# Spreading each expert's rows over the partitions, with two output accumulators and another gather order, in a mixture-of-experts layer step

## What is computed

```
scores = sigmoid(t @ w_router);  sel = scores + router_bias
top_e  = top 8 experts of each token, out of the 4 best of 8 groups
gates  = scores of the chosen 8, divided by their sum, times 2.5
for each of 64 experts:            # EXPERT_DIM = 256
    h   = silu(t @ wg) * (t @ wu)
    acc = acc + (h @ wd) * gate[:, None]
x = LN(ALPHA * x + acc + shared expert)
```

## Time and profile before

| | us |
|---|---|
| median of 3 runs | 1408.84 |
| lowest, highest | 1405.26, 1411.09 |
| the profiled execution | 1406.12 |
| its span, first to last instruction | 1404.4 |
| mean granted TensorE clock, of full speed | 0.945 |
| busy: PE / DVE / ACT / POOL | 1201.4 / 749.2 / 528.6 / 542.8 |
| HBM read, written | 324.71 MB, 49.74 MB |
| last scatter of the loop issued at | 1348.26 |

### The profile page before, as it was taken

How to read it: one execution, slowest core, us unless ns; L and a number is a source line. 1 busy time by engine, 2 the same in 40 slices (tenths; PEclk the granted TensorE clock), 3 DMA queues, 4 the chain that set the end, 5 groups by cost and what they waited for, 6 DMA issues and landing times. The chain is left out here.

```text
span 1404.4 us, 16199 instructions
## 1 busy us (share of the span) xinstructions
PE 1201.4 (86%) x6611; PEld 947.8 (67%) x6611; DVE 749.2 (53%) x925; ACT 528.6 (38%) x707; POOL 542.8 (39%) x352
## 2 busy tenths in 40 slices
PE   7999788899998999559998988999888888888930
PEld 6999567899998984247666666666666666666610
DVE  3125793532125435337666666666666666666637
ACT  3223672522223120044444444444444444444311
POOL 2001441210010203825555555555555555555413
PEclk9999896899999979879999999999999999999975
DMA  8930601122225075339899999989999988889741
GB/s 270 236 99 25 219 2 68 31 76 93 74 79 190 1 279 212 122 123 356 351 357 346 361 353 350 348 343 355 360 363 364 349 341 340 343 339 352 283 169 68
DMA packets 106017, 329.66 MB, mean 235 GB/s; under 512 B 26866, under 2 KB 59812, under 8 KB 80708
## 3 DMA queue, kind: packets, MB, share of 16 engines
q1 hardware_dynamic: 74848, 265.28, 50.8%
q0 software_dynamic: 30384, 63.02, 13.0%
q10 hardware_dynamic: 708, 0.28, 0.1%
HBM read 324.71 MB, written 49.74 MB: 267 GB/s over the span
## 5 line engine op out<-in xcount | busy, mean ns | idle before, releaser
L835 POOL DMA_INDIRECT yg<-y_rows,idx_all x64 | 259.2, 4050 | 162.7 <-DMA y_rows<-yg,idx_all 158.0
L1507 DVE TENSOR_TENSOR wgu_lo<-wgu,wgu_hi 128x4096 fp32r<-128x4096 f32 x64 | 282.7, 4417 | 0.0
L1122 ACT ACTIVATE wgu_hi<-wgu 128x4096 fp32r<-128x4096 f32 x63 | 227.8, 3616 | 53.7 <-DMA wgu<-in_w_up_e_dram 53.4
L1886 PE MATMUL bank<-wd,hT 128*128 128x512 f32 x512 | 230.1, 592 | 1.3 <-DVE yg L1519 1.3
L1867 PE MATMUL bank<-wgu_hi,xgT 128*128 128x512 f32 x512 | 206.8, 404 | 0.0
L1867 PE MATMUL bank<-wgu_lo,xgT 128*128 128x512 f32 x512 | 201.2, 393 | 0.0
L1867 PE MATMUL bank<-wgu_hi,xgT_lo 128*128 128x512 f32 x512 | 200.3, 391 | 0.0
L1886 PEld LDWEIGHTS bank<-wd,hT 128*128 128x128 f32 x512 | 96.7, 189 | 98.4 <-issue 92.0
L1519 DVE TENSOR_TENSOR yg<-yg,bank 128x512 f32<-128x512 f32 x128 | 82.2, 683 | 150.3 <-PE bank L1886 150.3
L1855 PE MATMUL bank<-ident,xg 128*128 128x128 f32 x512 | 75.7, 293 | 96.9 <-DMA xg<-x_rows,idx_all 94.8
L1499 DVE TENSOR_TENSOR xgT_lo<-bank,xgT 128x512 fp32r<-128x512 f32 x128 | 82.4, 686 | 141.7 <-ACT xgT L1116 141.7
(11 more groups left out here) (274 smaller groups left out, 2255.1 us busy)
## 6 DMA issues: line engine op xcount, KB each, us to landing
wgu<-in_w_gate_e_dram SPq DMA_DIRECT2D x64, 1024.0 KB, 10.5
wgu<-in_w_up_e_dram SPq DMA_DIRECT2D x64, 1024.0 KB, 20.3
wd<-in_w_down_e_dram SPq DMA_DIRECT2D x64, 1024.0 KB, 13.7
raw<-in_w_in_dram SPq DMA_DIRECT2D x16, 1024.0 KB, 6.2
y_rows<-sgln POOLq DMA_DIRECT2D x8, 512.0 KB, 7.1
raw<-in_w_proj_a_dram SPq DMA_DIRECT2D x4, 1024.0 KB, 5.0
raw<-in_w_out_dram SPq DMA_DIRECT2D x4, 1024.0 KB, 5.0
x_lo_kept<-xT_lo SPq DMA_DIRECT2D x1, 2304.0 KB, 10.2
```

What stands on the lines that cost most here:

```text
L835: pool.indirect_dma_start(out=yg[i][:], out_offset=None, in_=y_rows[i], in_offset=bass.IndirectOffsetOnAxis(idx, 0), bounds_check=bound, o ...
L1122: act.activation(wgu_hi[u % 2][:], wgu[u % WSLOTS][:], ACT.Copy).then_inc(hi_by_act, 1)
L1507: v.tensor_tensor(wgu_lo[u % WSLOTS][:], w_[:], wgu_hi[u % 2][:].bitcast(F32), ALU.subtract).then_inc(lo_by_dve, 1)
L1886: last = mm(bank[3 + h][:, :], hT[:, u % 2, j, :], wd[slot][:, j, h * 512:(h + 1) * 512], start=j == 0, stop=j == FE // P - 1)
```

## The change

Three things are changed together. The load of the list table reads place b x 16 + a into partition 8 a + b (`SPREAD = 16`), for the first tile on POOL in one DMA and for later tiles on SP in sixteen. There are two accumulators in place of three, and what belongs to the third is gone, by the constants alone: its zeroing, its buffer's memset, its read and its add. POOL's step is x gather of e+3, y gather of e, scatter of e-1.

```diff
-NACC = 3
+SPREAD = 16
+NACC = 2
...
+    spread = owner.rearrange("(t b a e) x -> t a b (e x)", t=NT, a=SPREAD, e=E)
...
-            rows = owner.rearrange("(t p e) a -> t p (e a)", t=NT, p=P)
...
-                    sp.dma_start(idx_all[:, :], rows[tile]).then_inc(idx_again, 16)
+                    for a in range(SPREAD):
+                        sp.dma_start(idx_all[a * P // SPREAD:(a + 1) * P // SPREAD, :], spread[tile][a]).then_inc(idx_again, 16)
...
-            pool.dma_start(idx_all[:, :], owner.rearrange("(t p e) a -> t p (e a)", t=NT, p=P)[0]).then_inc(idx_landed, 16)
+            pool.dma_start(idx_all[:, :], spread[0]).then_inc(idx_landed, 16)
...
             for e in range(E):
-                if e >= NACC:
-                    pool.wait_ge(y_put[acc[e]], 16 * (turn[e] - 1))
-                gather_y(acc[e], idx_all[:, e:e + 1])
                 n = e + XGSLOTS - 1
                 if n < E:
                     if e >= 1:
                         pool.wait_ge(h_by_dve, e)
                         pool.wait_ge(ex_xt, e)
                     gather_x(n % XGSLOTS, xg_in[n % XGSLOTS], idx_all[:, n:n + 1])
+                if e >= NACC:
+                    pool.wait_ge(y_put[acc[e]], 16 * (turn[e] - 1))
+                gather_y(acc[e], idx_all[:, e:e + 1])
                 if e >= 1:
                     pool.wait_ge(y_by_dve, 2 * e)
                     scatter_y(acc[e - 1], idx_all[:, e - 1:e])
...
-                    v.wait_ge(idx_again, 16 * tile)
+                    v.wait_ge(idx_again, 16 * SPREAD * tile)
```

## The result

The changed kernel takes **1586.66 us** (median of 4 runs, 1575.9 to 1596.23) against 1407.8 us: a ratio of 1.126, 95% interval 1.122 to 1.130. The forecast was 1395 us with a range to 1418. The profiled execution took 1596.23 us, its span is 1594.5 us. Lines of the kernel after are three higher.

The account below looks back on a forecast made before the run. The prediction took eight full DMA engines to bound the expert loop. Tail -12.2 and order -2 us, with spread and two accumulators at 0, summed to -14 us: 1408.8 to 1395 us, own range 1384 to 1403, for 8 in 10 1365 to 1418.

Parts of the forecast that it names:

- What bounds the kernel: Expert loop: eight full DMA engines need 11.46 us of the 11.53 us step; PE alone would need 10.29 us.
- the relief rival: Expert loop: the spread leaves at most 5 rows per engine, PE then bounds; 1325 us with the tail, chance 0.14 including partial.
- The spread: List places over partitions: load moves to other engines, eight still carry 8 rows; no gain, 0 us.
- The order: POOL's step: x gather issued earlier, PE's wait for it goes, weights are late next; -2 us.
- That costs no more than it does now: POOL's y gather, coming out after DVE's weight split behind the x gather, was to cost nothing extra.
- Two accumulators: Expert loop: chain of scatter, y gather and add fits two steps, 23.06 us, with landings of 12 to 20 us; 0 us.
- The slow rival: Expert loop: the two-accumulator chain binds with landings of 11.5 us each, step 12.85 us; 1474 us, chance 0.13.
- The x gather is the only thing that can be ahead: DMA queue in the loop: argument against long landings, with only the x gather in front of the y gather.
- The tail: DVE's work after the loop: five adds of the third buffer go; -12.2 us.

Follow-up runs that it names:

- the fours: Kernel before with another spread alone: first 64 places to partitions 0 to 31 and 64 to 95, the rest to the others; 1316.86 us, ratio 0.935.
- the old order: Kernel before with two accumulators alone, POOL still issuing scatter, y gather, x gather; 1487.83 us, ratio 1.057.
- the pause: Six small memsets holding POOL before each scatter: with two accumulators and POOL's order as before 1637.92 us, in the kernel before 1411.12 us.
- the scatter first: The changed kernel with POOL's order x gather, scatter of e-1, y gather of e; 1605.26 us, ratio 1.131.

## Why the prediction was wrong

**What bounds the kernel: right.** Eight full engines, 11.53 us a step. No row shows the load of a single engine, but relieving the eight brought the 6.5%, and PE was next, as said; the relief rival's 1325 us with its tail of 12 us in it compares with 1316.86 without: PE alone needs not 10.29 us a step but 10.0 at most.

**The spread: right, 0 us.** Ratio 0.999 alone, and the burst has the predicted 54 packets of six idle engines, with the 16 of two nearly idle ones behind them. The prediction rightly says that no row of the kernel before shows the rule of the Trainium skill, "DMA: Bandwidth & Descriptors", section "The descriptor swizzle", for an indirect transfer. The traces after it agree with the rule: 70 early small packets with the spread, none with the fours, which were laid out by its distance of 8.

**The order: right alone, as far as it can be told.** -2 us forecast, -6 [-9, -2] measured (0.4% of 1410, and the profiled execution does not show it), with the wait moved from PE to ACT's up weights as written. "That costs no more than it does now", of the y gather beside the split, was wrong in company: with three accumulators the y gather's length is on no chain, with two it is, at 3.19 for 1.34 us.

**Two accumulators: wrong, and this is the failed step.** The text has "it is queued on POOL ahead of the scatter of e-1" and then "must fit in two steps, 23.06 us", "so the two landings may add up to 20 us". The first sentence makes the second untrue. Data alone would allow two steps: the y gather of e needs the scatter of e-2. But the scatter of e-1 stands behind the y gather of e in POOL's order, and so inherits its wait: scatter of e-2, landing, y gather of e, scatter of e-1. One landing, not two, in one step, not two: landing + y gather + hand-over must be under 11.5 us. With the means of the kernel after, 11.1 + 3.1 + 0.6 (the idle time before the scatter) = 14.8 us, the step of 14.75 comes out. In the old order, with 9.0 us of landing, 1.3 of y gather, 1.6 of x gather and 1.2 of idle time before x gather and scatter, the chain is 13.1 us, and the step was 13.00: both over the full engines' 11.46. The gather's landing and the add, which the prediction put into the same chain, lie beside it. A second term was mis-sized: the sum took 6 to 10 us for each landing, and they were 11.6 and 12.0 us, 23.6 together. By the prediction's own chain that would be (23.6 + 2.7) / 2 = 13.2 us a step, and 14.66 was measured; so the size of the landings alone does not mend the forecast, and the kernel in the old order loses with landings of 16.5 us together, which that chain would let pass.

**The slow rival: right in sign, wrong in mechanism.** Its sign in the profile (DVE waits for the y gather, PE for the add) is there, but as a consequence of the late y gather. Its price was 30 us for each us of landing beyond; in a chain of one step it is 61 us over the 61 steps, and the pause, which added 1.68 us to the chain, lengthened the step by 2.46.

**"The x gather is the only thing that can be ahead": wrong.** The weights' burst is ahead or beside. Without seven eighths of a third of it the step is 2.8 us shorter, 1.1 us of it in the landing.

**The tail: right.** From the last y gather to the end 67.0 us before, 54.0 now. The five adds left take 1.21 to 1.23 us each:

```profile
L1569 DVE TENSOR_TENSOR x<-x,y_other x5: 1210/1218/1226, 1562.7 to 1579.8; 128x1024 f32<-128x1024 f32 x4, 64x1024 f32<-64x1024 f32 x1
```

**Not foreseen:** 11.9 us at the loop's start. 3.1 us of it lie before the first scatter (636.11 us for 633.00). The other 8.8 us are the new chain already: the y gather of expert 2 now waits for the scatter of expert 0 and starts 10.17 us after it, where it started 1.34 us after it.

```profile
646.28 0.99 POOL L838 DMA_INDIRECT yg<-y_rows,idx_all  x1 [7.81 <-DMA y_rows<-yg,idx_all]
```

## What to carry to other kernels

On an engine that works in order, a wait is inherited by everything behind it. Before taking away a buffer, write the engine's queue down and follow each wait forward: if the thing waited for next is issued behind the waiting instruction, the latency must fit in one period, however many buffers the data has. And where rows are moved by partition, count the packets of one transfer: balancing how many rows each DMA engine carries gave 6.5%, while spreading that kept the same eight engines deep gave nothing.

## What the runs showed of the hardware that was not expected

- A scatter lands in 3.2 us with nothing beside it (66 rows), and in 8.2 to 11.6 us (medians) in the kernels with two accumulators where the burst of 3 MB of weights comes near it, even where the DMA engines are idle for three tenths of the time. Where the burst came 3.6 us or more behind nearly every scatter (the scatter first), it landed in 3.3 us (median), though a y gather follows it after 1.3 us. Less of the burst shortens it (11.6 to 9.7 us).
- An issue of POOL's that meets DVE's 4.4 us weight split takes up to 5.2 us in place of 1.0, and in the lines shown it ends 0.9 us after the split does: the y gather in the kernel before and after, the x gather with the balanced fours (4.01 us at 1009.15). It costs time where the issue is on a chain, and none that was seen where POOL waits anyway.
- The mean granted TensorE clock from 700 to 1300 us was 0.99 before, with PE busy 535 of 600 us, and 0.87 after, with PE busy 477; with the balanced fours it was 1.00 with PE busy 500 of 500 us. At 0.87 PE is busy 11.7 us of a step of 14.66, so its speed does not set the step; no run tested what the clock would be without the gaps.
